# Softmax attention: both maxima of a turn ahead of the preceding turn's difference, the first scaling at the output

## What is computed

```python
def block(qi):                                   # 128 query rows; 528 keys
    s = jnp.einsum('bqhcd,bkhcd->bhcqk', qi, k)  # 4 heads h, 2 halves c of 64
    p = jax.nn.softmax(s, axis=-1)
    a = p[:, :, 0] - lam * p[:, :, 1]
    return jnp.einsum('bhqk,bkhv->bqhv', a, v)
```

## Time and profile before

| | |
|---|---|
| median of 3 runs | 2626.47 us (2623.98 to 2626.97) |
| span of the profiled execution | 2623.4 us |
| TensorE busy over the span | 2578.0 us (98%) |
| VectorE busy | 1529.6 us (58%) |
| ScalarE busy | 933.4 us (36%) |
| GpSimd busy | 1022.2 us (39%) |
| attention stage, about | 228 to 312 us |
| mean granted TensorE clock | 0.994 of full |

### The profile page before, as it was taken

One profiled execution on the slowest core, in us unless ns is written; L12 is line 12 of the kernel. 1 busy time (PEld: TensorE's weight loads), 2 busy tenths in 40 slices (PEclk: granted clock), 3 DMA queues, 4 the chain that ended last, 5 costly groups with the idle time before them and its releaser, 6 DMA issues.

```text
span 2623.4 us, 33878 instructions
## 1 busy us (share of the span) xinstructions
PE 2578.0 (98%) x12623; PEld 2119.2 (81%) x12623; DVE 1529.6 (58%) x3294; ACT 933.4 (36%) x1522; POOL 1022.2 (39%) x683
## 2 busy tenths in 40 slices
PE   8999999999999999999999999999999999999998
PEld 7886688888888888888888888877977788788887
DVE  3235738999688522225888888843984445433323
ACT  4224533333344322223333333353334442422222
POOL 3320010499888888605777777210360000000000
PEclk9999999999999999999999999999999999999999
DMA  4210156655656766658999999832332124333332
GB/s 149 80 33 33 58 164 205 213 126 143 138 132 187 199 146 146 146 167 302 372 371 370 373 370 369 307 105 81 81 91 63 41 81 136 84 98 98 99 97 72
DMA packets 330947, 427.89 MB, mean 163 GB/s; under 512 B 58720, under 2 KB 246912, under 8 KB 330272
## 3 DMA queue, kind: packets, MB, share of 16 engines
q1 hardware_dynamic: 271392, 358.39, 42.2%
q0 software_dynamic: 59392, 67.34, 10.5%
HBM read 362.59 MB, written 63.05 MB: 162 GB/s over the span
## 4 chain that ended last, share of the span: by engine, by line
PE 84%; ACT 1%; DVE 1%; issue 1%; DMA 0%; ACTq 0%; SPq 0%; DVEq 0%
PE bank L209 26%; PE bank L213 26%; PE bank L212 26%; PE bank L2692 1%; PE bank L1859 1%; PE bank L2667 1%; PE bank L1842 1%; PE bank L2650 0%; PE bank L2690 0%; PE bank L2680 0%; PE bank L563 0%; ACT s_wh L2399 0%; PE bank L2702 0%; ACT s_junk L2482 0%; PE bank L2749 0%
## 5 line engine op out<-in xcount | busy, mean ns | idle before, releaser
L1901 DVE TENSOR_TENSOR pe_wl<-pe_raw,pe_wh 128x1024 fp32r<-128x1024 f32 x270 | 351.6, 1304 | 367.8 <-ACT pe_wh L1757 352.7
L1687 POOL DMA_INDIRECT scratch_sums<-pe_pick,pe_cell_u x256 | 430.0, 1680 | 78.1 <-issue 77.8
L209 PE MATMUL bank<-pe_xh,pe_wh 128*128 128x512 f32 x1152 | 453.0, 393 | 1.1 <-DVE pe_xl L540 1.0
L213 PE MATMUL bank<-pe_xh,pe_wl 128*128 128x512 f32 x1152 | 448.6, 389 | 0.0
L212 PE MATMUL bank<-pe_xl,pe_wh 128*128 128x512 f32 x1152 | 448.4, 389 | 0.0
L1757 ACT ACTIVATE pe_wh<-pe_raw 128x1024 fp32r<-128x1024 f32 x270 | 285.8, 1059 | 303.4 <-PE bank L213 270.8
L2754 DVE TENSOR_TENSOR s_wl<-s_raw,s_wh 128x1024 fp32r<-128x1024 f32 x143 | 179.5, 1256 | 268.7 <-ACT s_wh L2399 267.4
L213 PE MATMUL bank<-pe_wh,pe_hl 128*128 128x512 f32 x768 | 298.8, 389 | 0.0
L209 PE MATMUL bank<-pe_wh,pe_hh 128*128 128x512 f32 x768 | 298.8, 389 | 0.0
L212 PE MATMUL bank<-pe_wl,pe_hh 128*128 128x512 f32 x768 | 298.8, 389 | 0.0
L213 PEld LDWEIGHTS bank<-pe_xh,pe_wl 128*128 128x128 f32 x1152 | 216.2, 188 | 45.6
(11 more groups left out here) (469 smaller groups left out, 4653.7 us busy)
## 6 DMA issues: line engine op xcount, KB each, us to landing
pe_raw<-in_peer_u SPq DMA_DIRECT2D x128, 512.0 KB
pe_raw<-in_peer_v SPq DMA_DIRECT2D x128, 512.0 KB
scratch_hidden<-pe_a_out SPq DMA_DIRECT2D x128, 256.0 KB
pe_a_in<-scratch_hidden SPq DMA_DIRECT2D x128, 192.0 KB
s_raw<-in_w_in SPq DMA_DIRECT2D x48, 512.0 KB, 3.9
s_raw<-in_w_gate_up SPq DMA_DIRECT2D x44, 512.0 KB, 3.9
scratch_sums<-pp_zeros SPq DMA_DIRECT2D x16, 1024.0 KB, 6.4
pe_added_gate<-scratch_sums SPq DMA_DIRECT2D x32, 512.0 KB
```

The lines of the kernel that those rows point to most:

```text
L209: first = pe.matmul(out, lhs[0], rhs[0], start=start, stop=False, skip_group_check=skip)
L213: return pe.matmul(out, lhs[1], rhs[0], start=False, stop=stop, skip_group_check=skip)
L1687: pool.indirect_dma_start(cells, bass.IndirectOffsetOnAxis(ap=cell_u[:, t, at:at + 1], axis=0), pick[:, t, 2, at:at + 1], None, compute_op ...
L1901: dve.tensor_tensor(wl[:, i % RING, :], raw[:, i % RAW, :], wh[:, i % RING, :].bitcast(F32), ALU.subtract).then_inc(S["w_lo"], 1)
```

## The change

On VectorE both maxima of turn r now stand ahead of the difference of turn r-1. The difference is no longer p0/sum0 + x·p1 but p0 + (x·sum0)·p1, with x the second reciprocal times `lam[:, 0:1]` (which holds the negated factor), and the missing 1/sum0 is applied to the output when it is taken from PSUM. So L1310 goes, L1311 becomes a product with two scalars, L1280 a product with one, and `inv` grows to eight turns, since the reciprocal is needed three turns later.

```diff
-        nmax, total, inv = s.sb("nmax", [P, 4]), s.sb("total", [P, 4]), s.sb("inv", [P, 4])
+        nmax, total, inv = s.sb("nmax", [P, 4]), s.sb("total", [P, 4]), s.sb("inv", [P, 8, 2])
...
                 dve.wait_ge(o_done, e + 1)
-                dve.tensor_copy(mix[:, t, hd * DA_V:(hd + 1) * DA_V], bank[:, O_BANK, 0:DA_V])\
-                    .then_inc(o_taken, 1)
+                dve.tensor_scalar(mix[:, t, hd * DA_V:(hd + 1) * DA_V], bank[:, O_BANK, 0:DA_V], inv[:, e % 8, 0:1], None,
+                                  ALU.mult).then_inc(o_taken, 1)
...
                 if r < len(turns):
                     maximum(r, 0)
+                    maximum(r, 1)
                 if 1 <= r <= len(turns):
                     e = r - 1
                     o = 2 * (e % 2)
                     dve.wait_ge(exped, 2 * e + 2)
                     if e >= 2:
                         dve.wait_ge(a_turned, e - 1)
-                    chain(dve.reciprocal(inv[:, o:o + 2], total[:, o:o + 2]))
-                    dve.tensor_scalar(a[:, e % 2, :], p[:, e % 2, 0, :], inv[:, o:o + 1], None, ALU.mult)
-                    chain(dve.tensor_tensor(inv[:, o + 1:o + 2], inv[:, o + 1:o + 2], lam[:, 0:1], ALU.mult))
-                    dve.scalar_tensor_tensor(a[:, e % 2, :], p[:, e % 2, 1, :], inv[:, o + 1:o + 2],
-                                             a[:, e % 2, :], ALU.mult, ALU.add).then_inc(diffed, 1)
-                if r < len(turns):
-                    maximum(r, 1)
+                    chain(dve.reciprocal(inv[:, e % 8, :], total[:, o:o + 2]))
+                    ratio = inv[:, e % 8, 1:2]
+                    chain(dve.tensor_scalar(ratio, ratio, total[:, o:o + 1], lam[:, 0:1], ALU.mult, ALU.mult))
+                    dve.scalar_tensor_tensor(a[:, e % 2, :], p[:, e % 2, 1, :], ratio, p[:, e % 2, 0, :], ALU.mult,
+                                             ALU.add).then_inc(diffed, 1)
```

## The result

| | before | changed |
|---|---|---|
| median of 5 runs | 2626.47 us (2623.98 to 2626.97) | 2609.28 us (2607.53 to 2610.41) |
| span of the profiled execution | 2623.4 us | 2607.4 us |
| first scores to the end of the last L1274 | 229.99 to 311.71, 81.7 us | 228.64 to 295.83, 67.2 us |

The ratio is 0.9936, with a 95% interval of 0.9925 to 0.9947: faster by 17.2 us, 0.65%. The five runs of the kernel before are the three of the first table and two more, with the same median. A second timing of the changed kernel, beside other runs of the kernel before, gave 2607.75 against 2626.29.

The account below looks back on a forecast made before the run. The prediction took TensorE, delayed in the attention stage by VectorE's order, as the bound. A 10.1 us gain up to turn 15's scores plus a shorter tail made 11.7: 2623.4 to 2611.7, plus 3.1 carried over, 2614.8, range 2608.5 to 2619.

Parts of the forecast that it names:

- VectorE's order costs 1.62 us every second turn: Attention stage: half 1's maximum waits behind the difference, delaying its next scores; moving it takes two turns from 8.29 to 6.9 us.
- What the removed scaling gives: VectorE queue: without L1310 the second maximum is held back 0.41 us less.
- The signs: Expected marks in clean turns: starts 3.3 to 3.6 apart, halves at most 0.25, maxima 0.62, shorter L1184 wait, L1312 ending early.
- The two-scalar product at 0.19 in the queue: VectorE's new one-column product: 0.19 us taken, as L1311, between bounds of 0.19 and 0.41.
- The difference's spare time: VectorE's difference, now behind both maxima, ends 0.86 us before the transposes that read it, so costs nothing.
- the bound of 5.5 us: Worst loss over three turns if GpSimd's L199 stalls the small product and L1312 on VectorE; at best 0.
- ScalarE's L192: Three instructions in turns 6 to 8 ahead of aT; with late VectorE maxima every fourth turn, 1.7 us added in all.
- The walk: Turn-by-turn sum of start times through the attention stage; turn 15's first scores at 283.2 at full clock, 298.00 before.
- the third case: Rival, chance 0.24: neither half-clock stretch of TensorE stays in the attention stage; gain 16.4 us, time 2610.1.
- The early stretch stays 10.2 us long and costs 4.7: TensorE in the attention stage: the early half-clock stretch remains, at 0.46 us per us; the second, short one goes.
- The last rival's side sum: Rival of a slower kernel, chance 0.04: half clock lasting to about 281 cancels the gain, to 292 loses 5.2 us.
- Carried over from the span: Whole kernel: the median's 3.1 us above the profiled span was added unchanged, taking 2611.7 to 2614.8.

Follow-up runs that it names:

- the order alone: Kernel before with only both maxima of a turn moved ahead of the preceding difference; L1310 stays, output copied unscaled: 2610.3 us, ratio 0.9938.
- both gaps filled: Kernel before with 14 unread transposes in TensorE's idle gaps, 9 ahead of turn 1's scores, 5 between turn 2's halves: 2621.54 us, ratio 0.9987.
- the filling of turn 2 alone: Kernel before with only 5 unread transposes between the halves of turn 2: 2626.76 us, ratio 1.0001.
- the scaling alone: Changed kernel with the second maximum back behind the difference; L1310 gone and the output scaled: 2621.63 us, ratio 0.9985.

## Why the prediction was right, and which terms were off

2614.8 was forecast, with a range of 2608.5 to 2619; 2609.28 was measured. The sign, the mechanism and the size of a turn were right; the clock was not. The gain was put at 11.7 us and is 17.2. It lies in the range because the range reaches down to the case in which no low clock stays; 2.7 us of it came from outside the stage, which is luck, and no term had foreseen them.

- *VectorE's order costs 1.62 us every second turn*: right. 6.9 us a pair were forecast and 6.88 measured, with halves at most 0.25 us apart, by the order alone too.
- *What the removed scaling gives*: right. 8.0 a pair was expected of it alone, 8.01 measured; in the whole change it is off the path.
- *The signs*: the starts of the turns (3.34 and 3.54), the halves (0.2) and the maxima (0.62) came as named. Two did not as worded. The wait of L1184 for L1288 was to fall by more than half, and 15.0 of 29.0 is a little less. The difference was to end before the next scores, and it ended 0.26 behind their start; the prediction's own sum, p+3.67 against p+3.34, had said so, and what counts, its readers, came later.
- *The two-scalar product at 0.19 in the queue*: too low. L1312 takes 273 ns, 0.31 to the next instruction; it lay between the bounds. *The output's scaling at 0*: 57 ns more than the copy (345 against 288), near the upper bound of 80. Both were hidden but in the last turns.
- *The difference's spare time* held: L1313 ended before the transposes asked for it, also where GpSimd stretched it to 1.44. No part of the bound of 5.5 us was paid.
- *ScalarE's L192*: 1.2 us for moving them away, of the 1.7 given to them and to the late fourth turns together.
- *The walk*: at full clock it gave the changed kernel a stage of 65.3 us (81.7 less the third case's 16.4); 65.8 were measured. For the kernel before it gave 77.8, which the expectation of the order alone names. The profile with both gaps filled has 77.9, with the stretch near 265 in it. The walk prices that stretch at 0.2, for which no row stands. An estimate from the timeline of the kernel before gives more: at full clock the scores of the turn at 268.87 would start at 268.16 (1.09 behind the product at 267.07, as in clean turns), and its second maximum at about 272.0 in place of 273.17. That is 1.2 us. So at equal clock the change is worth 10.9 to 11.9 us where the walk had 12.5.
- *The early stretch stays 10.2 us long and costs 4.7*: this step failed. A stretch of 3.4 us stood in its place. It cost 1.4 us (67.2 less 65.8), and the kernel before had lost 4.0 to 5.0 to its two (81.7 less 77.7 or 76.7). The clock thus gave 2.6 to 3.6 us where the sum had let it cost 0.8. The rival in which none stays, at 0.24 and 2610.1, came nearest, though one short stretch did stay. I had the reason for it, thinner turns ahead of each stretch, and put against it that 10 us of full busy time had not lifted the clock. That objection was worth less than I gave it: busy time counts a half score that runs alone as much as two that run together (this is argued; no run separates the two). By the Trainium skill ("TensorE: Matmul & The Clock Gate", What's actually happening) recent activity rules the clock; the two fillings together agree in sign, with 5 us less for 14 transposes more, while the filling of turn 2 alone moved no median. What decides whether a stretch stands at 234 or 240 stays open.
- *The last rival's side sum* doesn't close: with 0.46 a us, counted from 250.2, the gain of 11.7 is gone at 276 and 5.2 us are lost at 287, not at 281 and 292. Nothing else uses it.
- *Carried over from the span*: 1.35 us were gained ahead of the stage, which the change can't touch. The row of stretches from 30 to 50 shows why; first the kernel before, then the changed one:

```profile
30.00:50.00 20.00, 20.00 (x120) 16.24 (x119) 6.56 (x10) 4.15 (x5) 8.17 (x10) 0.91 0.38 113
```

```profile
30.00:50.00 20.00, 20.00 (x133) 16.23 (x132) 7.84 (x11) 5.03 (x7) 8.26 (x10) 1.00 0.39 119
```

  It was not the change: the second profile of the kernel before had 1.00 there and 0.66 from 90 to 100. And the 3.1 us between span and median were some 1.9 us around the span (1.8 to 2.1 in every run here) and 1.2 by which that execution was quicker than the median.
- The sum: 11.7, less 0.6 for the turns, plus 3.4 for the clock (or less 1.6 and plus 4.4), 1.4 around the stage and 1.2 for the median, makes 17.1 of the 17.2 measured.

## What to carry to other kernels

Where two chains of a software pipeline share an in-order engine, put the short instruction that another engine waits for ahead of the long one that has slack; that it is late shows in how far apart the partners start on the bound engine, not in busy time. Price such a change by the gap between two starts in clean turns, at equal clock, and hold the clock as a term of its own, for it follows the change. An idle gap of a pipeline's first turns may cost more behind it than in it, as the kernel before with both gaps filled suggests. Try to fill or close it, and time the result over many executions, since one profile can show the best of them, or one of the slowest.

## What the runs showed of the hardware

- Two products of 64 rows each, begun 0.2 us apart in different rows of the array, take 1.34 us together; one alone takes 1.12. The transposes behind them start 1.40 us after the first of the two, and 1.20 where both begin at once, so the 0.2 is all that the queue loses.
- TensorE stood at its lower level (0.50, 1.2 GHz) for 10 us while busy 2.00 us of every 2; 9 and 5 dead transposes in idle gaps ahead of it came with no such stretch in the profiled execution and with 5 us less in the median; 5 of them alone left the median as it was.
- The time was steady in the kernel before (all its runs lie from 2623.98 to 2627.83) and scattered in its filled variants (2620 to 2631) and with the scaling alone (2616 to 2627), with mean granted clocks from 0.991 to 0.997.
- A product of one column with two scalars per partition takes 273 ns on VectorE. L1311, with two inputs of the same size, takes 0.15 us undisturbed; its mean of 220 ns in the kernel before has GpSimd's hold of 1.22 us in it.
